# The low part of a step's weights: one VectorE operation behind both pieces of the high part

## The reference, cut to what matters

```python
h = rms_norm(x, norm_g)
u, v, z = jnp.split(h @ w_in, 3, axis=-1)          # layer A
...
x = x + y @ w_out
...
q, k, v, z, f_logit = jnp.split(h @ w_in, [...])   # layer B
...
x = x + y @ w_out
```

## Time and profile before

| | |
|---|---|
| median of 3 runs | 2214.89 us (2214.65 to 2216.71) |
| the profiled execution, its own time | 2215.99 us |
| its span, first to last instruction | 2214.2 us |
| PE busy | 2198.8 us, 99% |
| DVE / ACT busy | 1761.7 us, 80% / 1184.9 us, 54% |
| granted TensorE clock | 1.0 throughout |
| DMA | 249 GB/s mean |

### The profile page before, as it was taken

One profiled execution on the slowest core, in us unless ns is written; L12 is line 12 of the kernel. 1 busy time (PEld: TensorE's weight loads), 2 busy tenths in 40 slices (PEclk: granted clock), 3 DMA queues, 4 the chain that ended last, 5 costly groups with the idle time before them and its releaser, 6 DMA issues.

```text
span 2214.2 us, 27231 instructions
## 1 busy us (share of the span) xinstructions
PE 2198.8 (99%) x10150; PEld 1820.9 (82%) x10150; DVE 1761.7 (80%) x2152; ACT 1184.9 (54%) x1702; POOL 281.2 (13%) x381
## 2 busy tenths in 40 slices
PE   8999999999999999999999999999999999999999
PEld 6888888888888888888888888888888888888887
DVE  8978878877877877889798488976977888677666
ACT  6856655554554554565455565554564455443432
POOL 0011001001211211211200000110210210221100
PEclk9999999999999999999999999999999999999999
DMA  7788877879888888999997865686787797764333
GB/s 271 257 272 274 252 259 245 250 255 278 274 269 265 283 262 255 327 317 309 343 342 236 283 194 182 203 269 208 223 286 219 217 301 250 263 250 166 122 100 124
DMA packets 264628, 551.12 MB, mean 249 GB/s; under 512 B 22896, under 2 KB 39888, under 8 KB 263472
## 3 DMA queue, kind: packets, MB, share of 16 engines
q1 hardware_dynamic: 200096, 396.95, 56.0%
q0 software_dynamic: 37808, 104.16, 15.6%
q10 hardware_dynamic: 26592, 48.27, 5.7%
HBM read 449.60 MB, written 120.78 MB: 258 GB/s over the span
## 4 chain that ended last, share of the span: by engine, by line
PE 93%; DVE 4%; DMA 2%; issue 1%; ACT 1%; SPq 0%; ACTq 0%; POOL 0%; DVEq 0%
PE ps L1526 16%; PE ps L1519 16%; PE ps L1522 14%; PE ps L1493 9%; PE ps L1503 9%; PE ps L1498 9%; PE ps L1961 3%; PE ps L1959 3%; PE ps L1960 3%; PE ps L1859 2%; PE ps L1805 1%; PE ps L1531 1%; PE ps L1684 1%; PE ps L1732 1%; PE ps L1734 1%; PE ps L1733 1%
## 5 line engine op out<-in xcount | busy, mean ns | idle before, releaser
L970 ACT ACTIVATE u_hi<-raw 128x1024 fp32r<-128x1024 f32 x368 | 389.7, 1059 | 501.3 <-PE ps L1526 305.0
L2035 DVE TENSOR_TENSOR u_lo<-raw,u_hi 128x1024 fp32r<-128x1024 f32 x368 | 449.5, 1221 | 213.7 <-ACT u_hi L970 213.2
L977 ACT ACTIVATE u_hi<-raw 128x512 fp32r<-128x512 f32 (+1 forms) x368 | 311.3, 846 | 201.0 <-PE ps L1526 96.8
L2042 DVE TENSOR_TENSOR u_lo<-raw,u_hi 128x512 fp32r<-128x512 f32 (+1 forms) x368 | 349.9, 951 | 16.8 <-ACT u_hi L977 16.2
L1519 PE MATMUL ps<-u_hi,x1h 128*128 128x512 f32 x1056 | 283.0, 390 | 0.0
L1526 PE MATMUL ps<-u_lo,x1h 128*128 128x512 f32 x1056 | 282.5, 389 | 0.1
L1522 PE MATMUL ps<-u_hi,x1l 128*128 128x512 f32 x960 | 256.6, 389 | 0.0
L2010 DVE TENSOR_TENSOR raw<-raw 128x1024 f32<-128x1024 f32 x184 | 224.1, 1218 | 20.6 <-DMA raw<-in_b_w_in_dram 14.1
L1526 PEld LDWEIGHTS ps<-u_lo,x1h 128*128 128x128 f32 x1056 | 198.0, 188 | 41.9 <-DVE u_lo L2035 0.8
L1519 PEld LDWEIGHTS ps<-u_hi,x1h 128*128 128x128 f32 x1056 | 197.6, 188 | 40.8 <-ACT u_hi L970 0.2
L1522 PEld LDWEIGHTS ps<-u_hi,x1l 128*128 128x128 f32 x960 | 180.2, 188 | 37.4
(11 more groups left out here) (271 smaller groups left out, 3476.4 us busy)
## 6 DMA issues: line engine op xcount, KB each, us to landing
raw<-in_a_w_in_dram SPq DMA_DIRECT2D x280, 512.0 KB, 4.8
raw<-in_b_w_in_dram SPq DMA_DIRECT2D x184, 512.0 KB, 4.8
t_rows<-t ACTq DMA_DIRECT2D x184, 256.0 KB, 5.8
raw<-t_rows SPq DMA_DIRECT2D x184, 256.0 KB, 5.2
raw<-in_a_w_out_dram SPq DMA_DIRECT2D x72, 512.0 KB, 6.7
w_raw<-in_b_w_out_dram SPq DMA_DIRECT2D x64, 256.0 KB, 2.8
yf_rows<-y POOLq DMA_DIRECT2D x16, 512.0 KB, 5.2
yf_rows<-yf_rows POOLq DMA_DIRECT2D x64, 128.0 KB, 5.2
```

The costliest lines, as they stand in the source:

```text
L970: act.activation(first_tiles(hi), first_tiles(m), ACT.Copy).then_inc(hi1_first, 1)
L977: act.activation(other_tiles(hi, u, ph), other_tiles(m, u, ph), ACT.Copy).then_inc(hi1_ready, 1)
L2035: dve.tensor_tensor(first_tiles(lo), first_tiles(m), first_tiles(hi), ALU.subtract)\
L2042: dve.tensor_tensor(other_tiles(lo, u, ph), other_tiles(m, u, ph), other_tiles(hi, u, ph), ALU.subtract).then_inc(lo1_ready, 1)
```

## The change

`low_first` and `low_other` become one operation of the step's three or four tiles, behind `hi1_ready`, at the place where `low_other` stood. The semaphore `lo1_first` is gone; TensorE's wait ahead of the first half's `u_lo` matmuls is now on `lo1_ready`.

```diff
-        lo1_first = sem("lo1_first")
...
-                    two_products((pP, x1(k, a11, u), 2), (pX, x1(k, 0, u), 0), g, False, (lo1_first, g + 1), x_low)\
+                    two_products((pP, x1(k, a11, u), 2), (pX, x1(k, 0, u), 0), g, False, (lo1_ready, g + 1), x_low)\
...
-                mm = product(pP, *x1(k, a11, u), g, 2, one, end, low=(lo1_first, g + 1), x_low=x_low)
+                mm = product(pP, *x1(k, a11, u), g, 2, one, end, low=(lo1_ready, g + 1), x_low=x_low)
...
             def low(u, ph, k):
-                low_first(u, ph, k)
-                low_other(u, ph, k)
-
-            def low_first(u, ph, k):
                 g = step_of(u, ph, k)
-                hi, lo, m = u_hi[:, u_of(g), :, :].bitcast(F32), u_lo[:, u_of(g), :, :], raw_of(g)
-                dve.wait_ge(hi1_first, g + 1)
-                dve.tensor_tensor(first_tiles(lo), first_tiles(m), first_tiles(hi), ALU.subtract)\
-                    .then_inc(lo1_first, 1)
-
-            def low_other(u, ph, k):
-                g = step_of(u, ph, k)
+                n = width_of(u, ph)
                 hi, lo, m = u_hi[:, u_of(g), :, :].bitcast(F32), u_lo[:, u_of(g), :, :], raw_of(g)
                 dve.wait_ge(hi1_ready, g + 1)
-                dve.tensor_tensor(other_tiles(lo, u, ph), other_tiles(m, u, ph), other_tiles(hi, u, ph),
-                                  ALU.subtract).then_inc(lo1_ready, 1)
+                dve.tensor_tensor(lo[:, 0:n, :], m[:, 0:n, :], hi[:, 0:n, :], ALU.subtract).then_inc(lo1_ready, 1)
...
                 if k == 0:
-                    low_first(0, 0, 0)
                     x_low1(0)
                     sum_t2(0, 0)
-                    low_other(0, 0, 0)
+                    low(0, 0, 0)
...
                 for k in range(KP):
-                    if k > 1:
-                        low_first(u, 0, k)
                     if k + 1 < KP:
                         sums(u, 0, k + 1)
...
                     elif k > 1:
-                        low_other(u, 0, k)
+                        low(u, 0, k)
...
                 for k in range(KP):
-                    low_first(u, 1, k)
                     if k + 1 < KP:
                         sums(u, 1, k + 1)
                     elif u + 1 < NS:
                         sums(u + 1, 0, 0)
-                    low_other(u, 1, k)
+                    low(u, 1, k)
```

More of the change, by code:

```diff
@@ L1622, in second_half @@
                 if 0 < k < KP - 1 and not last:
-                    two_products((pP, x2(k, 0, u), 2), (pX, x2(k, a22, u), 0), g, True, (lo1_first, g + 1), x_low)\
+                    two_products((pP, x2(k, 0, u), 2), (pX, x2(k, a22, u), 0), g, True, (lo1_ready, g + 1), x_low)\
                         .then_inc(first_done, 1)
@@ L1632, in second_half @@
                     pe.wait_ge(e1_ready, u + 1)
-                mm = product(pP, *x2(k, 0, u), g, 2, False, end, True, low=(lo1_first, g + 1), x_low=x_low)
+                mm = product(pP, *x2(k, 0, u), g, 2, False, end, True, low=(lo1_ready, g + 1), x_low=x_low)
                 if end:
```

## The result

| | before | after |
|---|---|---|
| median | 2215.31 us (6 runs, 2214.24 to 2216.71) | 2229.56 us (6 runs, 2227.12 to 2230.16) |
| profiled execution, own time / span | 2215.99 / 2214.2 us | 2229.97 / 2228.2 us |

The ratio is 1.0058, with a 95% interval of 1.0048 to 1.0068: slower by 14.2 us where 10.9 were forecast, inside the range given. The profile moved in the same way, by 14.0 us of span. The same kernel was run again later, beside another set of runs of before. There the medians were 2227.22 against 2216.32, so 10.9 us, and its profiled execution took only 2223.99 us. Most of what follows is about the two places where those two executions part.

The account below looks back on a forecast made before the run. TensorE, busy 99% of the span, was taken as the bound. Places summed to 10.9 us (1.7 + 2.0 + 2.0 + 3.2 + 1.3 + 0.65), giving 2226.9 or 2225.8; forecast 2226.3 us, range 2221 to 2231.5.

Parts of the forecast that it names:

- The cost of one operation: VectorE's low part: 2.29 us for four tiles, 1.76 for three; busy time down by 25 to 55 us.
- The cover of ordinary steps: Most steps cost nothing: `u_lo` ends 3.5 us before TensorE loads it in phase 1, 1 to 3 in phase 0.
- Unit changes: Starts of units 2 to 13, 20 and 22: TensorE waits on L2146, 14 x 0.12 = 1.7 us.
- Unit 12: Step k = 3: ScalarE's second high part is late, so the operation ends after TensorE wants it; 2.0 us.
- Unit 22: Phase 1, k = 0: `sum_11` stands ahead of all of `u_lo`; 2.5 us late, less 0.5 no longer waited: 2.0.
- Unit 13: DMA-late step: the low part stands behind `sums` waiting for its load, ending 1081.2, wanted at 1079.94; 1.3 us.
- Unit 14: DMA-late step: the low part stands behind `sums` waiting for its load, ending 1156.6, wanted at 1155.73; 0.9 us.
- Unit 17: DMA-late step whose load is itself let go 1.06 us later; the low part ends 1498.3, wanted at 1497.28; 1.0 us.
- the third rival: Slower still, by loads let go later, in units 17, 19 and 21: 6.4 us more, 2233; chance 15%.
- Units 15 and 18: VectorE runs behind without a gap, so the operation ends after TensorE wants it; 0.6 + 0.7 = 1.3 us.
- The start: Low part of x: `u_lo` takes 1.76 us where 0.69 followed, delaying `x_sums1` and ScalarE's next copy; 0.65 us.
- TensorE's own figures: In the profile after, TensorE's busy time about as before and its idle time up by 11 us.

Follow-up runs that it names:

- safe: Changed kernel with two pieces again in units 0, 12 to 15, 17 to 19, 21, 22, one operation in the other thirteen; 2216.89 us, ratio 1.0002.
- only_u22: Kernel before, two pieces everywhere except one operation at step 0 of phase 1 of unit 22; 2219.1 us, ratio 1.0010.
- only_u12: Kernel before, two pieces everywhere except one operation at step 3 of phase 0 of unit 12; 2218.48 us, ratio 1.0008.
- u22_split: Changed kernel with two pieces again in phase 1 of unit 22, the first ahead of `sum_11`; 2228.0 us, ratio 1.0050.
- u13_load: Changed kernel with two pieces at step 1 of phase 0 of unit 13 alone, whose `lo1_ready` lets the late load go; 2228.91 us, ratio 1.0052.

## Why the prediction was right

Its range and its sign held, and its mechanism did: TensorE has no slack to give a stand back, VectorE has time to spare, so a later first `u_lo` costs wherever its cover is thin, and fewer operations earn nothing. The safe kernel shows the second half of that sentence by itself. By steps:

- **The cost of one operation**: 2.289 and 1.757 us, as taken. VectorE's busy time fell by 19.8 us; the forecast said 25 to 55. The durations of the `u_lo` operations alone fell by 54.9 us. But operations back to back overlap by some 0.08 us in the trace, and the busy time counts the overlap once: it was 134.4 us before and 102.1 after, with fewer operations and more of them behind a wait.
- **The cover of ordinary steps** held: in `safe`, 208 steps in one operation shift nothing between unit starts.
- **Unit changes**: 1.7 us forecast, 1.0 and 1.3 measured, but not as 14 x 0.12. Units 2 to 5 took 0.08 to 0.10 each, units 6 to 13 nothing, and unit 1, which I had counted among those that don't move, took 0.53: there TensorE waits 0.7 us for `eU` (L1492), the third operation of `sums_end` behind the long one. The margin of 0.11 us in the earlier trace rows was within what start times can tell, for eight units it was no wait. Of the 1.3 us, 0.37 is the start of unit 21, which came later by 0.11 and 0.17 us in `only_u22` and `only_u12` too, where all of units 20 and 21 is in two pieces.
- **Unit 12**: 2.0 forecast, 1.92 and 0.82 measured. The first is the sum as worked out. ScalarE's lateness in the earlier trace rows comes back in all profiles, but with the landing of a store that varied by 1.9 us; the ten profiles with one operation there give 0.8 to 2.7 us without the clock's part.
- **Unit 22**: the stand was worked out as 2.5 us on the loads and measured as 2.56 and 2.57; as a shift 2.0, measured 1.9 in the execution at full clock (2.08, less 0.16 at the next step) and 3.6 in the other. The 0.51 us ahead of the scores in the earlier trace rows, which the trace puts down to issue and the prediction to `sum_11`, are gone in both; in the code the scores do wait for it (`c11_ready`). What the prediction gave no thought to was the clock.
- **Unit 13**: the mis-sized term, 1.3 forecast and 4.31 measured in the profile shown with the result. The premise that failed is "start as L2042 at 1078.92": it took the load as landing where it did before. It was let go 0.87 us later, by the operation of step 1, and then landed 1.48 us later in one execution and 0.05 in the other, 0.96 in the mean of eight profiles against four. The prediction allowed 1 us for this in its upper end only. The rest, 1.6 to 1.7 us, is the clock.
- **Unit 14** 0.9 forecast, 0.93 and 0.85 measured. **Unit 17** 1.0 forecast, 0.25 and 0.06 measured: the load was issued 0.44 and 0.72 us later and not 1.06, and landed 0.35 and 0.16 later. It can do more: in the profile of `u22_split` it landed 1.75 us later, and the step cost 1.71. **Units 19 and 21**, where the same mechanism was not forecast, 0.49 and 0.40 in one execution, nothing in the other. With what unit 13 took over its forecast, which is the same mechanism, these two are all there is of the third rival: 0.9 us where it put 6.4.
- **Units 15 and 18**: 1.3 forecast at the two places, 1.5 measured in both profiles, and 0.45 more in the later steps of unit 18 in one. **The start**: 0.65 forecast, 0.9 and 1.2 measured, and 0.5 to 2.1 in the seven other profiles with one operation in unit 0, in a stretch where `safe`, with unit 0 as before, moves by 0.9 back and forth as well.
- **Given back**: 0.44 at the start of unit 14 and 0.8 to 1.0 at that of unit 15. But `safe` and `only_u22` gain 1.6 and 0.9 us at unit 15 without owing anything, and `only_u12` loses 0.9, so that start differs by execution and I don't count it as given back.
- **TensorE's own figures**: "busy time about as before, idle time up by 11" was 5.3 us busier and 8.7 more idle in the first profile, 3.4 and 4.6 in the second. A part of what a place costs is counted as busy: the matmuls at half clock, and about 0.3 us beside each stand on a late load.

The sum of 10.9 lies between the two profiles' 14.0 and 8.0. It is near the mean of both partly by luck: it had the clock at nothing and the unit changes and unit 17 too high.

The trace of one execution priced the places well and could not price their spread. The Trainium skill, Perfetto Trace Analysis, Optimizing Scalar/DVE Operations, says that breaking instructions up may let work complete sooner where an engine that is not saturated makes others wait. The runs agree where TensorE does wait: two operations in the same place took 0.53 us off the stand at unit 22, and two with the first ahead of the late `sums` took all of it off at unit 13. Where TensorE does not wait, one operation or two made no difference (`safe`, inside its units).

## What to carry to other kernels

Before two pieces are joined, ask what will stand in front of the first one's consumer: the joined operation inherits every wait of the last piece and of all that is queued between them, and that place costs more than the size (1.5 of 2.1 us at unit 22). If the engine that makes the pieces isn't the bound, the time saved on it buys nothing (here 10.9 us of VectorE for no change). A stand of TensorE of some 2 us can cost 1.7 times its length through the clock (3.71 us for 2.15), and a wait behind a DMA differs by 1 to 2 us from one execution to the next, so take several profiles before a place is priced by one.

## What the runs showed of the hardware

**The granted clock falls behind short stands of TensorE, in some executions.** Over the 13 profiles (that of before and twelve others), past the first 200 us, TensorE's matmuls stood 16 times for 1.86 to 2.41 us; behind 11 of these the clock was granted at 0.5 for 3.41 us, beginning between 0.1 us ahead of the stand's end and 1.4 us after it. Of 25 stands of 0.77 to 1.62 us one (1.15 us, at 1140.9 in `u13_load`) was followed by such a stretch, 1.8 us after its end. Stands of equal length (2.15 us at unit 22, in `only_u22` and in the changed kernel again) came out either way, so nothing in the length alone decides it. Each stretch cost 1.6 to 1.7 us at units 13 and 22, where it can be told from the stand. It is also one reason why runs lie a few us apart: the changed kernel's eleven runs go from 2223.99 us at a mean clock of 1.000 to 2232.04 at 0.997.

**A DMA's time differed by 1 to 2 us for the same bytes at the same place.** The load of step (13,0,5) was on its way for 15.33 to 16.76 us in the 13 profiles, and the store that ScalarE waits for in unit 12 landed within 1.9 us on the clock of before. Where such a transfer is late already, the variation went straight into TensorE's stand.
